# Recurrent gates of a two-block transformer kernel on one core: three products of rounded halves in place of one fp32 matmul

## The chip, the core and the metric

One core of a Trainium2 chip runs the whole program. It has five engines that work beside each other, each with its own queue of instructions, in order: TensorE (PE, matmul), VectorE (DVE), ScalarE (ACT), GpSimd (POOL) and SyncE (SP), the last two here used almost only to issue DMAs. The engines wait for each other by semaphores. The metric is the device time of one launch in microseconds (us), lower is better.

## The reference, cut to what matters

Two transformer blocks run over one sequence of 512 tokens and width 1024. The second one mixes tokens by dilated attention and by a gated linear recurrence of width 512, whose two gates are block-diagonal products (8 blocks of 64):

```python
def rg_lru(x, w_r, b_r, w_i, b_i, lam):
    xb = xf.reshape(b, s, N_LRU_BLOCKS, LRU_BLOCK)
    r = sigmoid(einsum('bsnc,ncd->bsnd', xb, w_r).reshape(b, s, c) + b_r)
    i = sigmoid(einsum('bsnc,ncd->bsnd', xb, w_i).reshape(b, s, c) + b_i)
    log_a = -LRU_C * r * softplus(-lam)
    a = exp(log_a)
    u = sqrt(-expm1(2.0 * log_a)) * (i * xf)
    _, h = associative_scan(combine, (a, u), axis=1)     # h = a * h_before + u
```

The input x of it is a projection of the normalised hidden state after a causal convolution of 4 taps. Everything is fp32.

## The kernel before, in words

Activations lie transposed: 128 features on the partitions, 512 tokens along them, so 1024 features are 8 such tiles. Weights stream from HBM in units of 128x1024 through a ring of four slots (`RING`). For each unit SyncE loads `w_raw`, ScalarE writes the rounded half `w_hi` and the negative of it, `w_lo` (lines 1025 and 1026, in `hi`, called by `ahead(name)` three units before the unit is used), and GpSimd adds `w_raw` onto `w_lo` by a DMA (line 514), so that `w_lo` is the remainder. Activations are split in the same way: ScalarE writes the rounded copy (type fp32r) and VectorE subtracts it from the source. `tile` (lines 545 to 547) then makes each fp32 product as three products of the rounded type: high by high, low by high, high by low. A tile of 8 pieces is 24 products into one of the two PSUM banks `pg`.

The stage of this case is the beginning of the second block's mixer. TensorE's order is written out by hand: the tiles xr0 to xr3 (512 recurrent features), each followed by the gate of the tile before it, then the attention tiles k2, q2, v2 of four head pairs with their scores. `lru_gate(t)` of TensorE (line 882) multiplies the convolved input `xc[:, t]` by a block-diagonal 128x128 piece for the r gate into bank `px` and by another for the i gate into bank `py`; both operands are plain fp32, and the matmul is not split. It waits for the third tap of the convolution (`xc_done`) and, on TensorE alone, for the weights of the gates (`l_landed`), which are 128x1024 (`lru_b`) and are loaded by a DMA from ScalarE's queue at line 1345, just ahead of the third norm's root.

Around it, for each t: VectorE multiplies the bank by the norm's root and frees it (line 1945), ScalarE makes the first tap (line 1357), VectorE the three others (line 1948). ScalarE's loop is at line 1354: the split of a later weight unit, the tap, and then, for t > 0, the sigmoids of gate t-1 (lines 1348 to 1352). The next `ahead` comes in the next turn of the loop. After gate 3 ScalarE and VectorE compute the factors and the scan (lines 1388 to 1393, 1951 to 1962), beside the first attention pair; `turn2` (line 904) is where TensorE needs VectorE's softmax of that pair. `statistic` (lines 599 to 606) sums squares for a norm. `put` (line 1474 of VectorE) adds a semaphore step to an instruction and has VectorE wait for it. SBUF buffers made in a closed `ExitStack` share their place with the ones made next.

Of the kernel before, what the change touches and what calls it, by code (L numbers as in the profile page):

```python
# [7 lines left out]
P = 128  # L8
T = 512
# [9 lines left out]
LRU_T = 512 // P  # L19
# [21 lines left out]
F32 = mybir.dt.float32  # L41
F32R = mybir.dt.float32r
BF16 = mybir.dt.bfloat16
ALU = mybir.AluOpType
ACT = mybir.ActivationFunctionType
# [148 lines left out]
def build(nc, weights, x_dram, consts, rope, masks, params, ssm_b, ssm_c, lru_w, out):  # L194
    with ExitStack() as ctx:
        def sb(name, shape, dt=F32, scope=ctx):
            return scope.enter_context(nc.sbuf_tensor(name, shape, dt))

        def sem(name):
            return ctx.enter_context(nc.semaphore(name))  # L200
# [72 lines left out]
        with ExitStack() as s:  # L273
            mx2_hi = sb("mx2_hi", [P, KT, T], F32R, scope=s)
            mx2_lo = sb("mx2_lo", [P, KT, T], F32R, scope=s)
            xc = sb("xc", [P, LRU_T, T], scope=s)
            tt = sb("tt", [P, LRU_T, T], scope=s)
            lru_b = sb("lru_b", [P, 2, LRU_T, P], scope=s)
            kk2 = sb("kk2", [P, 2, T], scope=s)
            qq2 = sb("qq2", [P, 2, T], scope=s)  # L280
            v_raw2 = sb("v_raw2", [P, T], scope=s)
            vv2 = sb("vv2", [P, QB, P], scope=s)
            prob2 = sb("prob2", [P, 6, T], scope=s)
            soft2 = sb("soft2", [P, 2, 8], scope=s)

# [56 lines left out]
        def psum(name, shape):  # L342
# [18 lines left out]
        c_landed, p_landed, s_landed, r_landed, l_landed, x2_landed = (  # L361
            sem(n) for n in ("c_landed", "p_landed", "s_landed", "r_landed", "l_landed", "x2_landed"))
# [14 lines left out]
        rs_k, rs_q, rs_o = sem("rs_k"), sem("rs_q"), sem("rs_o")  # L377
        cnv_act, silu_done, res_done = sem("cnv_act"), sem("silu_done"), sem("res_done")
        fin_mul, fin_pe, fin_act, fin_done = sem("fin_mul"), sem("fin_pe"), sem("fin_act"), sem("fin_done")
        xc_act, xc_done, la_done, tt_dve, tt_act, lru_h = (sem(n) for n in ("xc_act", "xc_done", "la_done", "tt_dve", "tt_act", "lru_h"))  # L380
        pv2_hi, cnv_done, gelu2_done, acc_done = sem("pv2_hi"), sem("cnv_done"), sem("gelu2_done"), sem("acc_done")

# [6 lines left out]
        def par(name, i=0):  # L389
            a, w = PARAMS[name]  # L390
            return prm[:, a + i:a + i + 1]

        def pars(name):
            a, w = PARAMS[name]
            return prm[:, a:a + w]
# [8 lines left out]
        def evacuated(eng, name):  # L404

            eng.wait_ge(pg_free[TILE[name] % 2], TILE[name] // 2 + 1)
# [10 lines left out]
        def ps_ready(eng, name):  # L417

            eng.wait_ge(ps_full, SUSE[name] + 1)
            return ps[SUSE[name] % 2]  # L420
# [107 lines left out]
        def _(pe):  # L528
# [242 lines left out]
            for h in range(1, HEADS + 2):  # L771
# [19 lines left out]
                if h >= 2:  # L791
# [4 lines left out]
                    for j in range(QB):  # L796
                        last = pe.matmul(py[:, P * j:T], vv[:, h % 2, j, :], pt[:, j, P * j:T],  # L797
                                         start=j == 0, stop=j == QB - 1)
# [83 lines left out]
            def lru_gate(t):  # L882
                for c, (bank, use, full, name) in enumerate(((px, x_use, px_full, "rg"), (py, y_use, py_full, "ig"))):
                    use((name, t))
                    if c == 0:
                        pe.wait_ge(xc_done, 3 * t + 3)
                        pe.wait_ge(l_landed, 16)
                    pe.matmul(bank[:], lru_b[:, c, t], xc[:, t], start=True, stop=True).then_inc(full, 1)

            for t in range(LRU_T):  # L890
                named(("xr", t), XH, XL, first_split=SPLIT["norm3"] if t == 0 else None, ahead_of=inside(3) if t == 0 else None)
                if t > 0:
                    lru_gate(t - 1)
# [39 lines left out]
            for j in range(PAIRS + 1):  # L933
                g = j - 1
                if j < PAIRS:
                    named(("k2", j), XH, XL)
                    if j == 0:
                        lru_gate(LRU_T - 1)
                    if j == 1:
                        value_turns(0)  # L940
# [67 lines left out]
        def _(act):  # L1008
            sent = {}

            def put(ins, s):

                ins.then_inc(s, 1)
                sent[s.name] = sent.get(s.name, 0) + 1
                return sent[s.name]
# [12 lines left out]
            def ahead(name):  # L1028
                hi(UNIT[name] + RING - 1)
# [8 lines left out]
            def px_ready(name):  # L1038
                act.wait_ge(px_full, XUSE[name] + 1)

            def py_ready(name):
                act.wait_ge(py_full, YUSE[name] + 1)
# [86 lines left out]
            for n, g in enumerate(GATES_FIRST):  # L1129
# [10 lines left out]
                if n == 10:  # L1140
                    for half in range(2):
                        use = ("y", half)
                        bank = ps_ready(act, use)
# [4 lines left out]
                if n == 11:  # L1148
                    for half in range(2):
                        use = ("yt", half)  # L1150
                        bank = ps_ready(act, use)
# [196 lines left out]
            def lru_gate(t):  # L1348
                px_ready(("rg", t))
                act.activation(ra[:, t], px[:], ACT.Sigmoid, bias=par("b_r", t)).then_inc(px_free, 1)  # L1350
                py_ready(("ig", t))
                act.activation(ii[:, t], py[:], ACT.Sigmoid, bias=par("b_i", t)).then_inc(py_free, 1)

            for t in range(LRU_T):
                ahead(("xr", t))
                evacuated(act, ("xr", t))
                put(act.activation(xc[:, t], sqr[:, t % 2], ACT.Identity, bias=par("cb2", t),
                                   scale=par("cw2", 12 + t)), xc_act)
                if t > 0:
                    lru_gate(t - 1)  # L1360

            def turned2(j, i):
                w = P * (i + 1)
                bank = ps_ready(act, ("t2", j, i))
                act.activation(pt2[i % 2][:, :, 0:i + 1, :], bank[:, :, 0:w].rearrange("p c (b q) -> p c b q", q=P), ACT.Copy)\
                    .then_inc(ps_free[SUSE[("t2", j, i)] % 2], 1)
# [106 lines left out]
        def _(dve):  # L1473
            sent = {}

            def put(ins, s):

                ins.then_inc(s, 1)
                sent[s.name] = sent.get(s.name, 0) + 1
                dve.wait_ge(s, sent[s.name])  # L1480
# [5 lines left out]
            def done(name):  # L1486
                dve.wait_ge(tile_done, TILE[name] + 1)
                return pg[TILE[name] % 2][:]

            def free(ins, name):  # L1490
                ins.then_inc(pg_free[TILE[name] % 2], 1)
                evacuated(dve, name)

            def tt_(out_, a, b, op=ALU.mult):
                return dve.tensor_tensor(out_, a, b, op)  # L1495

            def stt(out_, a, s, b, op0=ALU.mult, op1=ALU.mult):
                return dve.scalar_tensor_tensor(out_, a, s, b, op0, op1)  # L1498
# [442 lines left out]
            root_ready(3)  # L1941
            put(tt_(both[:], pars("mix_post"), pars("mlp_pre")), both_made)

            for t in range(LRU_T):
                free(tt_(sqr[:, t % 2], done(("xr", t)), rstd[:]), ("xr", t))
                dve.wait_ge(xc_act, t + 1)
                for d in (1, 2, 3):
                    put(stt(xc[:, t, d:T], sqr[:, t % 2, 0:T - d], par("cw2", 4 * (3 - d) + t), xc[:, t, d:T], ALU.mult,
                            ALU.add), xc_done)

            def lru_factor(t):

                dve.wait_ge(la_done, t + 1)
                link(tt_(nrm[:, t % 2], ra[:, t], ra[:, t]))
                put(stt(tt[:, t], nrm[:, t % 2], 1.0, tt[:, t], ALU.add, ALU.mult), tt_dve)
                py_read(dve, ("ig", t))
                link(tt_(ii[:, t], ii[:, t], xc[:, t]))
# [268 lines left out]
```

## Time and profile before

| | |
|---|---|
| median of 3 runs | 1428.45 us (1428.01 to 1429.33) |
| profiled execution | 1427.81 us |
| its span, first to last instruction | 1426.0 us |
| TensorE busy | 1402.4 us, 98% |
| ScalarE busy | 831.8 us, 58% |
| VectorE busy | 691.6 us, 48% |
| GpSimd busy | 197.7 us, 14% |
| mean DMA rate | 179 GB/s |

The profile is of one execution. The span is what its hardware profiler saw of instructions; 1.8 us of the execution's time lie around it. Matmuls are pipelined, so that the time of one row is longer than the distance to the next: the distance of two starts is what a matmul costs. An fp32 matmul appears as two instructions.

### The profile page before, as it was taken

To read this page: it belongs to the slowest core of one execution; us is meant where nothing else is said; L and a number is where in the kernel's file an instruction comes from. 1 tells how busy PE (TensorE), PEld (TensorE's weight loads), DVE (VectorE), ACT (ScalarE), POOL (GpSimd) and SP (SyncE) were. 2 spreads that over 40 slices of the span, in tenths; PEclk is the share of its full clock that TensorE was granted. 3 is DMA by queue.
4 is the path that set the end of the run, shared out by engine and by line. 5 is a ranking of instruction groups with operands and counts; after the bars stand their busy time and mean duration, and the time that the engine had idled before them with its cause. 6 is when DMAs were issued, how large, how long until landed. Compare 5 with 4: busy or idle time off the path is not lost.

```text
span 1426.0 us, 18304 instructions
## 1 busy us (share of the span) xinstructions
PE 1402.4 (98%) x6698; PEld 1118.5 (78%) x6698; DVE 691.6 (48%) x1211; ACT 831.8 (58%) x1169; POOL 197.7 (14%) x230
## 2 busy tenths in 40 slices
PE   7999999999999999999999999999999999999998
PEld 4887877777778888888888887777788888888885
DVE  6992567787733445554154164757464301212124
ACT  7546567776765665665355477645756655535442
POOL 1110110000111111111111111110101111111110
PEclk9999999999999999999999999999999999999999
DMA  9995976566479888888888996754667898988872
GB/s 295 199 209 152 209 168 146 126 154 142 115 186 230 188 195 190 194 190 198 203 186 187 216 239 151 159 140 110 144 152 162 192 208 180 201 198 181 203 161 85
DMA packets 81540, 254.76 MB, mean 179 GB/s; under 512 B 16688, under 2 KB 17840, under 8 KB 81456
## 3 DMA queue, kind: packets, MB, share of 16 engines
q0 software_dynamic: 32400, 117.98, 46.4%
q1 hardware_dynamic: 47616, 132.50, 30.7%
q10 hardware_dynamic: 1440, 3.15, 0.6%
q8 instruction: 54, 0.88, 0.2%
q14 instruction: 30, 0.25, 0.0%
HBM read 128.03 MB, written 3.41 MB: 92 GB/s over the span
## 4 chain that ended last, share of the span: by engine, by line
PE 93%; ACT 3%; DVE 3%; DMA 1%; issue 0%; SPq 0%; DVEq 0%; ACTq 0%
PE pg L545 27%; PE pg L547 27%; PE pg L546 27%; PE ps L719 2%; PE py L797 1%; PE ps L899 1%; PE ps L909 1%; ACT pairs_r L1189 1%; DMA w_raw<-weights 1%; PE py L919 1%; PE ps L721 0%; ACT kq_raw L1190 0%; PE ps L901 0%; DVE acc L1495 0%; DVE pairs L1495 0%
## 5 line engine op out<-in xcount | busy, mean ns | idle before, releaser
L545 PE MATMUL pg<-x_hi,w_hi 128*128 128x512 f32 x1088 | 429.2, 394 | 0.0
L547 PE MATMUL pg<-x_hi,w_lo 128*128 128x512 f32 x1088 | 424.2, 390 | 0.0
L546 PE MATMUL pg<-x_lo,w_hi 128*128 128x512 f32 x1088 | 423.7, 389 | 0.0
L514 POOL DMA_DIRECT2D w_lo<-w_raw x225 | 194.0, 862 | 1191.2 <-ACT w_lo L1026 1139.4
L1025 ACT ACTIVATE w_hi<-w_raw 128x1024 fp32r<-128x1024 f32 x222 | 233.4, 1051 | 107.6 <-PE pg L547 103.9
L545 PEld LDWEIGHTS pg<-x_hi,w_hi 128*128 128x128 f32 x1088 | 204.4, 188 | 43.2 <-issue 1.6
L547 PEld LDWEIGHTS pg<-x_hi,w_lo 128*128 128x128 f32 x1088 | 204.3, 188 | 42.9
L546 PEld LDWEIGHTS pg<-x_lo,w_hi 128*128 128x128 f32 x1088 | 204.5, 188 | 42.6 <-issue 1.0
L1026 ACT ACTIVATE w_lo<-w_raw 128x1024 fp32r<-128x1024 f32 x222 | 232.2, 1046 | 0.0
L547 PE MATMUL pg<-act_hi,w_lo 128*128 128x512 f32 x432 | 168.2, 389 | 0.0
L546 PE MATMUL pg<-act_lo,w_hi 128*128 128x512 f32 x432 | 168.1, 389 | 0.0
L545 PE MATMUL pg<-act_hi,w_hi 128*128 128x512 f32 x432 | 168.1, 389 | 0.0
L546 PEld LDWEIGHTS pg<-act_lo,w_hi 128*128 128x128 f32 x432 | 81.1, 188 | 16.9
L545 PEld LDWEIGHTS pg<-act_hi,w_hi 128*128 128x128 f32 x432 | 81.1, 188 | 16.8
L547 PEld LDWEIGHTS pg<-act_hi,w_lo 128*128 128x128 f32 x432 | 81.1, 188 | 16.7
L1495 DVE TENSOR_TENSOR pairs<-rel 128x512 f32<-128x512 f32 x30 | 20.8, 692 | 134.5 <-ACT rel L1448 134.5
L1495 DVE TENSOR_TENSOR cu<-pg,rstd 128x512 f32<-128x512 f32 x44 | 30.4, 692 | 114.6 <-PE pg L547 112.9
L1495 DVE TENSOR_TENSOR hid<-hid,pg 128x512 f32<-128x512 f32 x32 | 22.0, 688 | 102.8 <-PE pg L547 98.3
L1498 DVE SCALAR_TENSOR_TENSOR cnv<-cu,prm,cnv 128x511 f32<-128x511 f32 x88 | 66.1, 751 | 3.1
L1495 DVE TENSOR_TENSOR acc<-acc,pg 128x512 f32<-128x512 f32 x24 | 16.5, 688 | 96.1 <-PE pg L547 96.1
L1169 ACT ACTIVATE pr<-ps,soft 128x128 f32<-128x128 f32 (+3 forms) x64 | 33.2, 523 | 27.2 <-DVE soft L1779 26.5
L1779 DVE TENSOR_REDUCE soft<-ps 128x2 f32<-128x256 f32 (+3 forms) x48 | 39.6, 824 | 6.7 <-PE ps L901 4.1
(355 smaller groups left out, 1711.7 us busy)
## 6 DMA issues: line engine op xcount, KB each, us to landing
w_raw<-weights SPq DMA_DIRECT2D x226, 512.0 KB, 5.0
w_lo<-w_raw POOLq DMA_DIRECT2D x225, 512.0 KB, 5.8
kq_rot<-kq_raw SPq DMA_DIRECT2D x64, 64.0 KB, 3.1
hid<-x SPq DMA_DIRECT2D x4, 512.0 KB, 5.5
hid<-x ACTq DMA_DIRECT2D x8, 256.0 KB, 5.3
out<-hid SPq DMA_DIRECT2D x8, 256.0 KB, 2.2
u_dram<-hid SPq DMA_DIRECT2D x4, 256.0 KB, 5.2
pairs<-u_dram SPq DMA_DIRECT2D x8, 128.0 KB, 8.1
```

What stands on the lines that cost most here:

```text
L514: pool.dma_start(w_lo[:, s], w_raw[:, s], accum_op=ALU.add).then_inc(lo_in[s], 16)
L545: pe.matmul(bank[:], wh, xh(k), start=n == 0, stop=False)
L546: pe.matmul(bank[:], wh, xl(k), start=False, stop=False)
L547: last = pe.matmul(bank[:], wl, xh(k), start=False, stop=n == len(ks) - 1)
L719: pe.matmul(bank[:, c, 0:w], qq[r, h % 2, P * i:P * i + P], kk[r, h % 2, 0:w], start=True, stop=False)
L797: last = pe.matmul(py[:, P * j:T], vv[:, h % 2, j, :], pt[:, j, P * j:T], start=j == 0, stop=j == QB - 1)
L1025: act.activation(w_hi[:, s], w_raw[:, s], ACT.Copy)
L1026: put(act.activation(w_lo[:, s], w_raw[:, s], ACT.Copy, scale=-1.0), hi_done)
L1169: ins = act.activation(dst[:, c, 0:w], bank[:, c, 0:w], ACT.Exp, bias=negmax[:, i % 2, c:c + 1], **kw)
L1495: return dve.tensor_tensor(out_, a, b, op)
L1498: return dve.scalar_tensor_tensor(out_, a, s, b, op0, op1)
L1779: put(dve.tensor_reduce(s[:, i % 2, 0:2], bank[:, :, 0:w], AX.X, ALU.max, negate=True), maxed)
```

## The change

It adds split halves of the gate weights, `lb_hi` (rounded copy, ScalarE) and `lb_lo` (remainder, VectorE), made once ahead of the loop over t, and split halves of the gate input, `xc_hi` and `xc_lo`, made for each t in two alternating buffers. The four fit into places of buffers that are filled later (`qq2`, `prob2`). TensorE's gate is three products of the rounded type for each of r and i. `wait_ge(l_landed, 16)` moves from TensorE to ScalarE, ahead of `lb_hi`; VectorE waits for `lb_hi` ahead of its evacuation of xr0; ScalarE waits for the third tap of each t ahead of `xc_hi`, and VectorE for `xc_hi` ahead of `xc_lo`, which TensorE waits for.

```diff
--- before.py
+++ after.py
@@ -277,9 +277,15 @@
             tt = sb("tt", [P, LRU_T, T], scope=s)
             lru_b = sb("lru_b", [P, 2, LRU_T, P], scope=s)
             kk2 = sb("kk2", [P, 2, T], scope=s)
+            with ExitStack() as s2:
+                lb_lo = sb("lb_lo", [P, 2, LRU_T, P], F32R, scope=s2)
             qq2 = sb("qq2", [P, 2, T], scope=s)
             v_raw2 = sb("v_raw2", [P, T], scope=s)
             vv2 = sb("vv2", [P, QB, P], scope=s)
+            with ExitStack() as s2:
+                xc_hi = sb("xc_hi", [P, 2, T], F32R, scope=s2)
+                xc_lo = sb("xc_lo", [P, 2, T], F32R, scope=s2)
+                lb_hi = sb("lb_hi", [P, 2, LRU_T, P], F32R, scope=s2)
             prob2 = sb("prob2", [P, 6, T], scope=s)
             soft2 = sb("soft2", [P, 2, 8], scope=s)
 
@@ -377,6 +383,7 @@
         rs_k, rs_q, rs_o = sem("rs_k"), sem("rs_q"), sem("rs_o")
         cnv_act, silu_done, res_done = sem("cnv_act"), sem("silu_done"), sem("res_done")
         fin_mul, fin_pe, fin_act, fin_done = sem("fin_mul"), sem("fin_pe"), sem("fin_act"), sem("fin_done")
+        lb_high, lb_low, xc_high, xc_low = sem("lb_high"), sem("lb_low"), sem("xc_high"), sem("xc_low")
         xc_act, xc_done, la_done, tt_dve, tt_act, lru_h = (sem(n) for n in ("xc_act", "xc_done", "la_done", "tt_dve", "tt_act", "lru_h"))
         pv2_hi, cnv_done, gelu2_done, acc_done = sem("pv2_hi"), sem("cnv_done"), sem("gelu2_done"), sem("acc_done")
 
@@ -883,9 +890,11 @@
                 for c, (bank, use, full, name) in enumerate(((px, x_use, px_full, "rg"), (py, y_use, py_full, "ig"))):
                     use((name, t))
                     if c == 0:
-                        pe.wait_ge(xc_done, 3 * t + 3)
-                        pe.wait_ge(l_landed, 16)
-                    pe.matmul(bank[:], lru_b[:, c, t], xc[:, t], start=True, stop=True).then_inc(full, 1)
+                        pe.wait_ge(lb_low, 1)
+                        pe.wait_ge(xc_low, t + 1)
+                    pe.matmul(bank[:], lb_hi[:, c, t], xc_hi[:, t % 2], start=True, stop=False)
+                    pe.matmul(bank[:], lb_hi[:, c, t], xc_lo[:, t % 2], start=False, stop=False)
+                    pe.matmul(bank[:], lb_lo[:, c, t], xc_hi[:, t % 2], start=False, stop=True).then_inc(full, 1)
 
             for t in range(LRU_T):
                 named(("xr", t), XH, XL, first_split=SPLIT["norm3"] if t == 0 else None, ahead_of=inside(3) if t == 0 else None)
@@ -1351,6 +1360,8 @@
                 py_ready(("ig", t))
                 act.activation(ii[:, t], py[:], ACT.Sigmoid, bias=par("b_i", t)).then_inc(py_free, 1)
 
+            act.wait_ge(l_landed, 16)
+            put(act.activation(lb_hi[:], lru_b[:], ACT.Copy), lb_high)
             for t in range(LRU_T):
                 ahead(("xr", t))
                 evacuated(act, ("xr", t))
@@ -1358,6 +1369,8 @@
                                    scale=par("cw2", 12 + t)), xc_act)
                 if t > 0:
                     lru_gate(t - 1)
+                act.wait_ge(xc_done, 3 * t + 3)
+                put(act.activation(xc_hi[:, t % 2], xc[:, t], ACT.Copy), xc_high)
 
             def turned2(j, i):
                 w = P * (i + 1)
@@ -1941,12 +1954,16 @@
             root_ready(3)
             put(tt_(both[:], pars("mix_post"), pars("mlp_pre")), both_made)
 
+            dve.wait_ge(lb_high, 1)
+            put(tt_(lb_lo[:], lru_b[:], lb_hi[:].bitcast(F32), ALU.subtract), lb_low)
             for t in range(LRU_T):
                 free(tt_(sqr[:, t % 2], done(("xr", t)), rstd[:]), ("xr", t))
                 dve.wait_ge(xc_act, t + 1)
                 for d in (1, 2, 3):
                     put(stt(xc[:, t, d:T], sqr[:, t % 2, 0:T - d], par("cw2", 4 * (3 - d) + t), xc[:, t, d:T], ALU.mult,
                             ALU.add), xc_done)
+                dve.wait_ge(xc_high, t + 1)
+                put(tt_(xc_lo[:, t % 2], xc[:, t], xc_hi[:, t % 2].bitcast(F32), ALU.subtract), xc_low)
 
             def lru_factor(t):
```

## Rows read from the trace of the kernel before

**Rows 1.** one line of the page, part 1: busy us, share, instructions.

```profile
PE 1402.4 (98%) x6698; PEld 1118.5 (78%) x6698; DVE 691.6 (48%) x1211; ACT 831.8 (58%) x1169; POOL 197.7 (14%) x230
```

**Rows 2.** the page, part 4: the chain that ended last.

```profile
PE 93%; ACT 3%; DVE 3%; DMA 1%; issue 0%; SPq 0%; DVEq 0%; ACTq 0%
PE pg L545 27%; PE pg L547 27%; PE pg L546 27%; PE ps L719 2%; PE py L797 1%; PE ps L899 1%; PE ps L909 1%; ACT pairs_r L1189 1%; DMA w_raw<-weights 1%; PE py L919 1%; PE ps L721 0%; ACT kq_raw L1190 0%; PE ps L901 0%; DVE acc L1495 0%; DVE pairs L1495 0%
```

**Rows 3.** timeline of TensorE: start us, us, engine, line, [idle before].

```profile
855.63 0.39 PE L546 MATMUL pg<-x_lo,w_hi 128*128 128x512 f32 x1
855.86 0.39 PE L547 MATMUL pg<-x_hi,w_lo 128*128 128x512 f32 x1
856.09 1.02 PE L888 MATMUL px<-xc,lru_b 128*128 128x512 f32 x2
...
863.30 1.02 PE L888 MATMUL px<-xc,lru_b 128*128 128x512 f32 x2
```

**Rows 4.** timeline of ScalarE, same columns.

```profile
850.18 0.63 ACT L1074 ACTIVATE rstd<-rstd 128x512 f32<-128x512 f32 x1
850.72 1.04 ACT L1025 ACTIVATE w_hi<-w_raw 128x1024 fp32r<-128x1024 f32 x1
851.66 1.04 ACT L1026 ACTIVATE w_lo<-w_raw 128x1024 fp32r<-128x1024 f32 x1
...
857.09 0.81 ACT L1357 ACTIVATE xc<-pairs,prm 128x512 f32<-128x512 f32 x1 [1.77 <-DVE pairs L1495]
857.92 1.28 ACT L1350 ACT_TABLE_LOAD   x1
859.21 0.69 ACT L1350 ACTIVATE acc<-px,prm 128x512 f32<-128x512 f32 x1
```

**Rows 5.** timeline of VectorE, same columns.

```profile
847.88 0.69 DVE L1495 TENSOR_TENSOR pairs_r<-rstd,pairs_r 128x512 fp32r<-128x512 f32 x1
...
851.11 0.69 DVE L1495 TENSOR_TENSOR pairs<-pg,rstd 128x512 f32<-128x512 f32 x1
853.51 2.32 DVE L1498 SCALAR_TENSOR_TENSOR xc<-pairs,prm,xc 128x511 f32<-128x511 f32 x3 [1.71 <-ACT xc L1357]
...
858.00 2.32 DVE L1498 SCALAR_TENSOR_TENSOR xc<-pairs,prm,xc 128x511 f32<-128x511 f32 x3 [0.95 <-ACT xc L1357]
```

**Rows 6.** load of the gate weights: timeline of ScalarE's queue, view of line 1345.

```profile
847.16 0.33 ACTq L1345 DMA_DIRECT2D lru_b<-lru_w  x1
...
DMA to landing us min/median/max: 5.7/5.7/5.7
```

**Rows 7.** the view of line 1558: duration ns min/median/max, start, shape.

```profile
L1558 DVE TENSOR_TENSOR w_lo<-w_raw,w_hi x1: 1224/1224/1224, 12.7 to 12.7; 128x1024 fp32r<-128x1024 f32 x1
```

**Rows 8.** timeline of both engines at the recurrent split.

```profile
923.79 0.63 ACT L1047 ACTIVATE mx_hi<-pairs 128x512 fp32r<-128x512 f32 x1 [0.83 <-DVE pairs L1495]
...
924.53 0.69 DVE L1495 TENSOR_TENSOR mx_lo<-pairs,mx_hi 128x512 fp32r<-128x512 f32 x1 [0.77 <-ACT mx_hi L1047]
```

**Rows 9.** timeline of TensorE at the third norm's sum.

```profile
848.72 0.47 PE L604 MATMUL px<-pairs_r,blocks 128*128 128x512 f32 x1 [0.33 <-DVE pairs_r L1495]
849.02 0.40 PE L605 MATMUL px<-pairs_r,blocks 128*128 128x512 f32 x1
```

**Rows 10.** the view of w_lo: its 225 additions by DMA.

```profile
DMA to landing us min/median/max: 4.5/5.8/12.0
```

**Rows 11.** waits of TensorE: us in total, times, longest.

```profile
PE ps L909 <- DVE prob L1501: 0.7, 1, 0.7
```

**Rows 12.** timeline of TensorE at the start.

```profile
11.39 1.02 PE L622 MATMUL px<-gates 128*128 128x512 f32 x2
...
17.00 0.77 PE L561 MATMUL pg<-x_hi,w_hi 128*128 128x512 f32 x1 [2.65 <-DVE x_lo L1495]
```

**Rows 13.** stretches at the start: busy us by engine, then granted clock, DMA share.

```profile
12.50:16.00 3.50, 0.35 (x2) 0.30 (x2) 2.76 (x4) 2.85 (x7) 0.00 (x0) 1.00 1.04 415
16.10:22.80 6.70, 5.80 (x14) 4.57 (x15) 6.39 (x10) 6.70 (x11) 1.86 (x2) 0.50 1.05 311
```

## The prediction

> **What bounds the kernel now.** I read the busy times first: TensorE is busy for 1402.4 of 1426.0 us [rows 1]. The chain that ended last says the same: 93% of it is TensorE, 81 of the 93 on the three lines that multiply by streamed weights, 3% is ScalarE and 3% VectorE [rows 2]. So a microsecond of matmul taken out of TensorE's queue is worth a microsecond, and a microsecond in which TensorE is made to wait costs one. The other two views are therefore TensorE's own order of instructions around the gates, and the order on ScalarE and VectorE that leads up to the first gate. TensorE runs tile xr0, tile xr1, gate 0, tile xr2, gate 1, tile xr3, gate 2, tile k2_0, gate 3. The last product of xr1 is issued at 855.86, gate 0 follows at 856.09 with no idle time [rows 3]. That this works is close: the third convolution tap of t = 0 starts at 853.51 + 2 steps and ends at 853.51 + 2.32 = 855.83 [rows 5], 0.26 us before the gate wants it. Gates 1 to 3 have room: the taps of t = 1 end at 858.00 + 2.32 = 860.32 and gate 1 starts at 863.30 [rows 3, 5].
>
> **What the matmuls give back.** One period from gate 0 to gate 1 is 863.30 - 856.09 = 7.21 us [rows 3]. In it lie the 24 products of one tile. Neighbouring products are 0.227 us apart (855.63, 855.86, 856.09) [rows 3], so the tile takes 24 x 0.227 = 5.45 us and the fp32 gate 1.76 us (two fp32 matmuls, each two instructions). The new gate is six products of the kind of the tile: 6 x 0.227 = 1.36 us. Saved: 0.40 us per gate, four gates, 1.6 us, all on the path while TensorE doesn't wait. The rule of the Trainium skill (FP8 and Floating Point Precision, TensorE Precision Notes) is that a true fp32 product is four passes, high and low halves each with each; three of four would save 1.76 / 4 x 4 = 1.8 us. The rows give 1.6, and I go by them; an instruction pair per matmul in the trace doesn't contradict it.
>
> **What the splits cost, step by step, for t = 0.** This is where the change can hurt, since before it gate 0 had 0.26 us of slack and four new operations and one new wait now stand ahead of it in series. I lay them out in time, taking everything up to the third root (exponential done at 850.81 [rows 4]) as unchanged.
> - *The wait for the gate weights.* Before, only TensorE waited for `l_landed`, at 856. Now ScalarE does, directly behind the root, and everything later in its queue stands behind it. The transfer is issued at 847.16 and lands 5.7 us later, at 852.86 [rows 6]. ScalarE, which before went on at 850.72 with the weights of the next tile [rows 4], idles for 2.1 us. Queued behind are the split of two weight tiles, the first tap and the gates' sigmoids.
> - *lb_hi*, 128x1024 on ScalarE: the same shape as the weight copy, 1.04 us [rows 4]: 852.86 to 853.91.
> - *The weight copies of ahead(xr0)*, 0.95 us apart [rows 4]: to about 855.85. They finish before the first tap has its input, so they cost nothing here.
> - *lb_lo*, 128x1024 on VectorE: the one such operation in the trace took 1224 ns [rows 7]; with 0.1 us of handover from ScalarE, 854.0 to 855.25. VectorE stands at it from 851.1 on, and queued behind it is the evacuation of xr0, which before ran at 851.11 [rows 5].
> - *Evacuation*, 0.69: to 855.97. *First tap on ScalarE* and its handover: 857.09 to 858.00 in the row of t = 1 [rows 4, 5], 0.91: VectorE's taps start at 856.93. *Three taps*, 2.32: to 859.25.
> - *xc_hi on ScalarE, xc_lo on VectorE.* The nearest pair is the split of the recurrent output: ScalarE starts at 923.79, VectorE at 924.53 for 0.69 [rows 8]. From the end of the taps: 0.04 + 0.74 + 0.69 = 1.47: to 860.72. TensorE starts 0.15 behind such an end (847.88 + 0.69 = 848.57, matmul at 848.72) [rows 5, 9].
>
> So gate 0 starts at 860.9 in place of 856.1: TensorE stands for 4.8 us where it stood for none. To this I add 0.1 us for the slower first products behind a wait (848.72 to 849.02, 0.30 in place of 0.23) [rows 9]. Of the 4.9 the wait for the transfer carries 2.1: had the gate weights been there at 850.81, the same steps would begin and end 2.05 us earlier and gate 0 would start at 858.8.
>
> **The later gates.** t = 1 on ScalarE: xc_hi(0) ends at 859.95, then the weight copies to 861.95, the tap (its input from VectorE is ready at 861.6) with handover to 862.85, VectorE's taps to 865.2, the pair to 866.65, TensorE ready at 866.8. TensorE ends gate 0 at 860.9 + 1.4 = 862.3 and xr2 at 867.75. 0.9 us of slack. The sigmoids of gate 0 with their table load, 1.28 + twice 0.69 [rows 4], run from 862.75 to 865.3, beside the taps, and xc_hi(1) is queued just behind them; the slack holds this. For t = 2 and 3 the input comes when the tile ends, and from there to its own gate VectorE and ScalarE need 0.7 (evacuation) + 0.9 (tap, handover) + 2.3 (taps) + 1.5 (the pair) + 0.15 = 5.6 us. TensorE meanwhile has the gate before, 1.36, and the next tile, 5.45, which is 6.8: 1.2 us of slack. Without that cover each gate would wait by the difference.
>
> **Weights, DMA queues.** ScalarE's delay moves the split of xr3's weights from 852.7 to 855.85 and that of k2_0's from 855.3 to 861.95. GpSimd issues the addition behind each, SyncE the next load behind that. An addition lands after 5.8 us in the median and 12.0 at most [rows 10]: xr3's at 862 to 868, wanted at 869.2; k2_0's at 868 to 874, wanted at 876. No cost, but at the far end 1 us of room only.
>
> **Downstream.** Behind gate 3 the chain goes over ScalarE and VectorE to the turns of the first pair, where TensorE waits 0.70 us [rows 11]. That chain begins with the sigmoids of gate 3, which move with TensorE (gate 3 is 0.4 us shorter for both sides), so that wait stays as it is: it neither swallows the new stall nor grows. The reuse of the two buffers of xc_hi and xc_lo is two gates apart and waits for nothing.
>
> **The sum.** 4.9 - 1.6 = +3.3 us. The profiled execution took 1427.81 us, 1.8 around its span of 1426.0; by it, 1431.1. The median of the runs shown is 0.6 above it, 1428.45, which gives 1431.8. Bounds of the unshown parts: landing 0.5 us earlier or later (it shares the DMA engines with weight traffic), handovers 0.3 us in all, which makes 2.5 to 4.2 us.
>
> **Rival one: the clock falls in the gap.** TensorE's granted clock is full everywhere in this part. The one place where the trace shows it fall is the start. The last 512-column matmul there begins its pair at 11.39 and ends at 12.41, then come two short ones, busy for 0.35 us together, and real work starts at 17.00 [rows 12, 13]. The granted clock is 1.00 up to 16.0 and 0.50 from 16.1 to 22.8, though TensorE was busy for 5.8 of these 6.7 us [rows 13], that is at 1.2 of 2.4 GHz. This cost half of 5.8, 2.9 us. The new gap of 4.8 us is as long as that one (4.6) and emptier. Against it: one instance only, behind a thin start, and here the engine was fully busy up to the gap. If it falls, the price is from near 0 to 3.3 us, by how much of the slow stretch lies inside the gap; I take the row's 2.9, which gives 1431.8 + 2.9 = 1434.6. It hides nowhere, since TensorE is the bound. The Trainium skill (TensorE: Matmul & The Clock Gate, HAM oscillation — how this bites in real kernels) has the rule that idle gaps between bursts of matmuls send the clock to its lower level and the next burst starts cold; the start of this trace agrees.
>
> **Rival two, on the other side: the gap isn't there and the kernel is faster.** The mechanism would be that the data of gate 0 are ready by 856.1, so that the 1.6 us of matmul time is all that is left: 1428.45 - 1.6 = 1426.9. It decides from a chain shorter by 4.8 us; the landing can give 2.1, and the rest would need two of the four new operations to overlap, which their semaphores don't allow. What speaks for it is only that the landing is a single row.
>
> **Rival three: the transfer lands early.** If ScalarE finds the gate weights there at 850.81, the stall is 2.7 + 0.1 and the change +1.2 us: 1429.6, no change that can be told. That asks for 3.7 us, while the additions, of the same 512 KB, never took less than 4.5 [rows 10], so it isn't likely.
>
> **How the numbers follow.** A measurement of this kernel can tell some 0.2%, 2.9 us, from no change, so 1431.3 is the border. The stall with the clock kept, 1431.8 (1430.9 to 1432.7): 0.46; of it three quarters lie over the border, 0.34, and 0.12 under. The stall with the clock falling, 1434.6 (1432 to 1435.6): 0.38, all over. Early landing, 1429.6: 0.10, same. No gap, 1426.9: 0.06, faster or same by half. Slower 0.72, same 0.25, faster 0.03. The range leaves out the no-gap case and half of the early landing: 1430.1 to 1435.4.
>
> **What would show it.** Right: a row of TensorE's gate matmul with idle time of 4 to 5 us ahead of it at t = 0 and none at t = 1 to 3; lb_hi on ScalarE starting at 852.9 with the landing as its releaser; gate periods of 5.45 + 1.36 = 6.8 us in place of 7.21; the 0.70 us wait of the first turn unchanged. The clock: the mean granted clock of the stretch behind the gap, and products 0.43 us apart there. Wrong: a second stall at gate 1 (ScalarE's queue fuller than laid out), a wait for weights at xr3 or k2_0, or a chain that TensorE doesn't stand for.

## The result, and the profile after

| | before | changed |
|---|---|---|
| median of 5 runs | 1428.15 us (1427.66 to 1429.33) | 1435.09 us (1433.31 to 1436.51) |
| profiled execution, span | 1427.81, 1426.0 | 1435.09, 1433.3 |
| ratio to before | | 1.0046, 95% interval 1.0036 to 1.0057 |

The change makes the kernel 6.9 us slower. The forecast of 1431.8 had the sign and the place, and its range of 1430.1 to 1435.4 holds the median, but the size was half of what came. The measured value is that of the first rival, 1434.6: the gap with the clock falling in it. How far that agreement is luck is said further down.

The page of the changed kernel, the busy time of TensorE and the chain that ended last (before in rows 1 and 2). Lines 545 to 547 of before are now 552 to 554, ScalarE's and VectorE's lines move too:

```profile
PE 1402.6 (98%) x6702; PEld 1120.1 (78%) x6706; DVE 695.3 (49%) x1216; ACT 835.5 (58%) x1174; POOL 197.7 (14%) x230
...
PE 90%; ACT 4%; DVE 3%; DMA 2%; issue 1%; SPq 0%; DVEq 0%; ACTq 0%
PE pg L552 27%; PE pg L554 26%; PE pg L553 26%; PE ps L726 2%; PE py L804 1%; PE ps L908 1%; PE ps L918 1%; ACT pairs_r L1198 1%; DMA w_raw<-weights 1%; DMA w_lo<-w_raw 1%; PE py L928 1%; DMA lru_b<-lru_w 0%; PE ps L728 0%; ACT kq_raw L1199 0%; DVE pairs L1508 0%
```

TensorE is busy for 0.2 us more than before although eight fp32 matmuls (two for each gate) have become cheaper. The busy time counts slow work and much work alike, so the saving and the slow clock cancel in it. Its share of the chain is down from 93% [rows 2] to 90%, and the load of the gate weights has appeared in the chain. Where it stands shows in TensorE's order around the gates (timeline, columns as in rows 3):

```profile
856.46 0.39 PE L554 MATMUL pg<-x_hi,w_lo 128*128 128x512 f32 x1
862.73 0.77 PE L895 MATMUL px<-xc_hi,lb_hi 128*128 128x512 f32 x1 [5.88 <-DVE xc_lo L1508]
863.29 0.63 PE L896 MATMUL px<-xc_lo,lb_hi 128*128 128x512 f32 x1
...
866.71 0.62 PE L552 MATMUL pg<-x_hi,w_hi 128*128 128x512 f32 x1
867.13 0.42 PE L553 MATMUL pg<-x_lo,w_hi 128*128 128x512 f32 x1
867.40 0.39 PE L554 MATMUL pg<-x_hi,w_lo 128*128 128x512 f32 x1
...
871.75 0.39 PE L895 MATMUL px<-xc_hi,lb_hi 128*128 128x512 f32 x1
...
878.54 0.39 PE L895 MATMUL px<-xc_hi,lb_hi 128*128 128x512 f32 x1
```

The last product of xr1 starts at 856.46 and gate 0 at 862.73: 5.88 us of idle time, where there was none [rows 3]. The six products of the gate and the first five of xr2 behind it are 0.43 us apart (as 866.71 to 867.13; the first step, 862.73 to 863.29, is longer still); after one step of 0.27 they are 0.23 apart again. From 862.73 to 867.40 there are 11 steps in 4.67 us, where 11 x 0.227 would be 2.50: 2.2 us lost. Gate 1 and gate 2 start at 871.75 and 878.54 without a wait, 6.79 us apart where it was 7.21 [rows 3].

Stretches of the changed kernel (busy us of each engine, then the granted clock, DMA share, GB/s), the gap's first half, the stretch behind and the one after:

```profile
857.00:860.00 3.00, 0.00 (x0) 0.00 (x0) 1.98 (x4) 1.50 (x2) 0.86 (x1) 1.00 0.23 44
860.50:867.20 6.70, 4.47 (x11) 3.55 (x12) 4.26 (x6) 6.01 (x8) 0.86 (x1) 0.50 0.74 168
867.50:874.00 6.50, 6.50 (x30) 5.34 (x29) 1.73 (x3) 3.14 (x4) 0.86 (x1) 1.00 0.68 153
```

The granted clock is 1.00 for the first part of the gap, 0.50 from 860.5 to 867.2, 1.00 after: 1.2 in place of 2.4 GHz. So it fell some 4 us after the last product of xr1 was issued, inside the gap, and 4.5 us of work ran at it. Before the change the only such stretch was at the start [rows 13].

Why gate 0 is late, from ScalarE's and VectorE's timelines of the changed kernel:

```profile
847.75 0.34 ACTq L1354 DMA_DIRECT2D lru_b<-lru_w  x1
...
850.76 0.63 ACT L1083 ACTIVATE rstd<-rstd 128x512 f32<-128x512 f32 x1
854.74 1.06 ACT L1364 ACTIVATE lb_hi<-lru_b 128x1024 fp32r<-128x1024 f32 x1 [3.34 <-DMA lru_b<-lru_w]
855.71 1.04 ACT L1034 ACTIVATE w_hi<-w_raw 128x1024 fp32r<-128x1024 f32 x1
856.65 1.04 ACT L1035 ACTIVATE w_lo<-w_raw 128x1024 fp32r<-128x1024 f32 x1
857.89 0.81 ACT L1368 ACTIVATE xc<-pairs,prm 128x512 f32<-128x512 f32 x1 [0.20 <-DVE pairs L1508]
861.16 0.63 ACT L1373 ACTIVATE xc_hi<-xc 128x512 fp32r<-128x512 f32 x1 [2.46 <-DVE xc L1511]
```

```profile
855.90 1.23 DVE L1508 TENSOR_TENSOR lb_lo<-lru_b,lb_hi 128x1024 fp32r<-128x1024 f32 x1 [4.24 <-ACT lb_hi L1364]
857.16 0.69 DVE L1508 TENSOR_TENSOR pairs<-pg,rstd 128x512 f32<-128x512 f32 x1
858.80 2.32 DVE L1511 SCALAR_TENSOR_TENSOR xc<-pairs,prm,xc 128x511 f32<-128x511 f32 x3 [0.95 <-ACT xc L1368]
861.89 0.69 DVE L1508 TENSOR_TENSOR xc_lo<-xc,xc_hi 128x512 fp32r<-128x512 f32 x1 [0.77 <-ACT xc_hi L1373]
```

These are the steps of the forecast in their order: the root ends at 851.39, ScalarE idles for 3.34 us until the gate weights land; then come lb_hi, lb_lo, the evacuation of xr0, the taps, xc_hi and xc_lo. The one step that differs in size is the first, the landing. The load was issued at 847.75 and took this long (view of its line):

```profile
DMA to landing us min/median/max: 7.0/7.0/7.0
```

7.0 us, where the trace of before had 5.7 [rows 6].

TensorE's waits in the changed kernel, in total, times and longest:

```profile
PE px L895 <- DVE xc_lo L1508: 5.9, 1, 5.9
...
PE ps L918 <- DVE prob L1514: 0.7, 1, 0.7
...
PE pg L552 <- DMA w_lo<-w_raw: 0.5, 1, 0.5
```

The wait of the first turn, 0.7 us, is what it was [rows 11]. A wait of 0.5 us for an addition to `w_lo` is new, but it lies at 836.44, ahead of anything that the change touches. Two kernels below that are the same as before up to this point have a wait of 0.6 us there too, so it comes and goes between executions. It accounts for most of the 0.6 us by which the starts near 850 are late against before. The span then adds up: 6.0 (856.69 to 862.73) + 2.2 (clock) - 1.6 (four times 0.4) + 0.5 = 7.1, measured 1433.3 - 1426.0 = 7.3.

### The profile page after: what moved, and what is told of

Read it like the earlier page. It is cut to its first block, busy times and chain, and to the rows that moved or that the text cites. A ratio compares the mean times of both kernels' runs of the same rounds, so it can differ in the third digit from the quotient of the medians.

```text
span 1433.3 us, 18331 instructions
## 1 busy us (share of the span) xinstructions
PE 1402.6 (98%) x6702; PEld 1120.1 (78%) x6706; DVE 695.3 (49%) x1216; ACT 835.5 (58%) x1174; POOL 197.7 (14%) x230
## 4 chain that ended last, share of the span: by engine, by line
PE 90%; ACT 4%; DVE 3%; DMA 2%; issue 1%; SPq 0%; DVEq 0%; ACTq 0%
PE pg L552 27%; PE pg L554 26%; PE pg L553 26%; PE ps L726 2%; PE py L804 1%; PE ps L908 1%; PE ps L918 1%; ACT pairs_r L1198 1%; DMA w_raw<-weights 1%; DMA w_lo<-w_raw 1%; PE py L928 1%; DMA lru_b<-lru_w 0%; PE ps L728 0%; ACT kq_raw L1199 0%; DVE pairs L1508 0%
```

## The experiments

The theory after the result had three terms: three products for one fp32 matmul save 1.6 us; a gap before gate 0 costs 6 us, of which the wait for the gate weights is over half and the series of splits the rest; the clock falls in the gap and costs 2.2 us more. The rivals: the products save nothing in place; the landing is hidden and the splits alone make the gap; the clock falls for another reason or its fall costs nothing. What the nine kernels gave is below. Landing, gap and clock are those of one profiled execution each (landing: issue to landing of the gate weights; gap: end of xr1's last product to the start of gate 0). The last column is the median of before from the same group of runs; each ratio further down is against it.

| kernel | landing, us | gap, us | clock behind the gap | median, us | before beside it |
|---|---|---|---|---|---|
| before | 5.7 | 0 | full | 1428.15 | |
| changed | 7.0 | 6.0 | half | 1435.09 | 1428.15 |
| changed, again | 7.5 | 6.6 | half | 1435.45 | 1428.11 |
| products alone | 6.8 | 0 | full | 1426.51 | 1428.06 |
| wait alone | 7.1 | 3.4 | half | 1433.74 | 1428.06 |
| splits alone | 7.8 | 6.9 | half | 1437.06 | 1428.11 |
| gap filled | 7.5 | 6.6, 4.6 of it filled | full | 1432.67 | 1428.06 |
| load early | in time | 2.6 | full | 1429.10 | 1428.06 |
| splits early | in time | 1.2 | full | 1427.65 | 1428.11 |
| splits early, gate 0 later | in time | 0 | full | 1426.44 | 1428.11 |

**Products alone.** Before, with the products of the gates on other operands:

```diff
-                    pe.matmul(bank[:], lru_b[:, c, t], xc[:, t], start=True, stop=True).then_inc(full, 1)
+                    wt, xt = blocks[:, c], x_hi[:, t]
+                    pe.matmul(bank[:], wt, xt, start=True, stop=False)
+                    pe.matmul(bank[:], wt, xt, start=False, stop=False)
+                    pe.matmul(bank[:], wt, xt, start=False, stop=True).then_inc(full, 1)
```

> The kernel before, with each fp32 gate matmul replaced by three products of the rounded type on other tiles that are already rounded (the ones tile and x_hi); the gates are not computed, the waits are those of before. It prices the matmul part alone. Theory: gate period 5.45 + 1.36 = 6.81 us in place of 7.21, no stall, so 1.6 us less than before: 1426.5. Rival (the three products are no cheaper in place, for example because each brings its own weight load and the fp32 one hides it): 1428.1, period 7.2.

Measured: 1426.51 (1425.78 to 1427.40, 11 runs) against 1428.06, ratio 0.9989, interval 0.9980 to 0.9998. Its timeline of TensorE has the gates at

```profile
857.00 0.39 PE L889 MATMUL px<-x_hi,blocks 128*128 128x512 f32 x1
...
863.83 0.39 PE L889 MATMUL px<-x_hi,blocks 128*128 128x512 f32 x1
```

6.83 us apart, and there is no wait for a gate. The saving is 1.55 us as summed. The rival falls: its period was 7.2, and its time, that of before, lies just outside the interval.

**The wait alone.** Before, plus one line on ScalarE:

```diff
             inverse_root(3, rstd)
 ...
+            act.wait_ge(l_landed, 16)
             for t in range(LRU_T):
                 ahead(("xr", t))
```

> The kernel before, with nothing but a wait for the gate weights added on ScalarE ahead of its loop over the recurrent tiles; no split is made and the fp32 gates stay. Theory that the landing is a main part of the stall: ScalarE idles 2 to 3.3 us, tap 0 is late by as much, TensorE stands 1.9 to 3.2 us ahead of gate 0 (0.26 us of slack taken off, 0.8 us gained or lost by the weight copies), 1430 to 1431.5, clock kept. Rival (the split operations alone make the stall, the landing is hidden): within 0.3 us of before.

Measured: 1433.74 (1431.25 to 1434.51), ratio 1.0036, interval 1.0022 to 1.0049. The landing isn't hidden; the wait alone costs 5.7 us, more than I had expected. ScalarE's timeline:

```profile
855.00 1.06 ACT L1025 ACTIVATE w_hi<-w_raw 128x1024 fp32r<-128x1024 f32 x1 [3.46 <-DMA lru_b<-lru_w]
...
856.92 0.80 ACT L1358 ACTIVATE xc<-pairs,prm 128x512 f32<-128x512 f32 x1
```

TensorE's:

```profile
856.60 0.39 PE L547 MATMUL pg<-x_hi,w_lo 128*128 128x512 f32 x1
860.24 2.02 PE L888 MATMUL px<-xc,lru_b 128*128 128x512 f32 x2 [3.25 <-issue]
...
863.96 0.39 PE L546 MATMUL pg<-x_lo,w_hi 128*128 128x512 f32 x1
```

The weight copies that stood at 850.72 [rows 4] start at 855.00 and the first tap at 856.92. The gap is 856.83 to 860.24, 3.4 us, with a landing of 7.1; 3.2 was the most that was expected. The larger miss is the clock, which I had taken as kept: from 860.24 to 863.96 the gate and one product take 3.72 us, where the same took 858.03 - 856.09 = 1.94 in the kernel before [rows 3], whose second product of xr2 is

```profile
858.03 0.40 PE L546 MATMUL pg<-x_lo,w_hi 128*128 128x512 f32 x1
```

3.4 + 1.8 = 5.2. The rest of this execution's 5.9 us (its span is 1431.9) is mostly a wait of 0.6 us for an addition at 836.55, as in the changed kernel. So a gap of 3.4 us was long enough here to meet the fall. The five runs lie in two places: 1431.3 and 1431.8, where the gap with a full clock would put them (1428.06 + 3.4 = 1431.5), and 1433.7 to 1434.5. That the clock was kept in the lower two is likely but not shown; only a run of the upper group has a trace.

**The gap filled.** The changed kernel, with work that nobody reads ahead of gate 0's wait:

```diff
                     use((name, t))
+                    if c == 0 and t == 0:
+                        for _ in range(20):
+                            pe.matmul(bank[:], blocks[:, 0], x_hi[:, 0], start=True, stop=True)
                     if c == 0:
                         pe.wait_ge(lb_low, 1)
```

> The changed kernel, with 20 products of 0.227 us (4.5 us in all) on tiles at hand put ahead of the first gate's wait, into the gate's own bank, where the first gate overwrites them: TensorE works in the gap and the gap's end isn't moved. Theory that the gap makes the granted clock fall: the clock stays full, products behind the gate stay 0.227 us apart, 1435.1 - 2.3 = 1432.8. Rival (the clock falls for another reason, or its fall costs nothing because the next gate waits anyway): 1435.1.

Measured: 1432.67 (1431.31 to 1433.36, 7 runs), ratio 1.0033, interval 1.0021 to 1.0044. TensorE's timeline and the stretches:

```profile
855.86 4.70 PE L894 MATMUL px<-x_hi,blocks 128*128 128x512 f32 x20
862.42 0.47 PE L898 MATMUL px<-xc_hi,lb_hi 128*128 128x512 f32 x1 [1.86 <-DVE xc_lo L1511]
862.72 0.40 PE L899 MATMUL px<-xc_lo,lb_hi 128*128 128x512 f32 x1
```

```profile
856.00:862.00 6.00, 4.55 (x21) 3.43 (x19) 4.18 (x6) 3.35 (x5) 0.86 (x1) 1.00 0.46 87
862.40:869.00 6.60, 6.58 (x29) 5.50 (x30) 3.54 (x5) 6.57 (x9) 0.86 (x1) 1.00 0.70 159
```

Gate 0 is as late as in the changed kernel (862.42, and here the gate weights took 7.5 us), but the clock is 1.00 throughout, and the gate's products are 0.30 and then 0.23 apart. 2.4 us come back by adding 20 matmuls (2.8 against the second measurement of the changed kernel, whose gap is as long, 6.6 us). All seven runs are at or below 1433.36, all ten of the changed kernel at or above 1433.31. This shows that it is the idle time that lets the clock fall, and that the fall costs 2.4 to 2.8 us by the medians. The sum for the changed kernel agrees: 1428.15 + 6.0 + 2.2 - 1.6 = 1434.8, measured 1435.09.

This is also the case in which gate 1 stands under a full clock: its xc_lo ends at 867.97 and it starts at 869.31 without a wait. The slack that the forecast gave the later gates is there, and not a gift of the slow clock.

**The load early.** The changed kernel, with the DMA moved to the first of the last eight tiles of the feed-forward:

```diff
                             evacuated(act, ("down", c, m))
+                            if m == 0:
+                                act.dma_start(lru_b[:], lru_w).then_inc(l_landed, 16)
                             square(3, m, hid[:, m])
 ...
-            act.dma_start(lru_b[:], lru_w).then_inc(l_landed, 16)
             inverse_root(3, rstd)
```

> The changed kernel, with the load of the gate weights issued some 30 us earlier, behind the first of the last eight tiles of the feed-forward, so that ScalarE never waits for it. Theory: lb_hi starts at about 850.8, the gap before gate 0 is 2.7 us, the clock is kept: 1428.2 + 2.8 - 1.6 = 1429.4. Rival (the gap comes from the chain of splits, and an earlier landing only moves the wait): gap near 6 us, 1435.

Measured: 1429.10 (1428.62 to 1430.80, 11 runs), ratio 1.0010, interval 1.0001 to 1.0019. ScalarE and TensorE:

```profile
850.14 0.63 ACT L1083 ACTIVATE rstd<-rstd 128x512 f32<-128x512 f32 x1
850.68 1.04 ACT L1365 ACTIVATE lb_hi<-lru_b 128x1024 fp32r<-128x1024 f32 x1
```

```profile
855.83 0.39 PE L554 MATMUL pg<-x_hi,w_lo 128*128 128x512 f32 x1
858.65 0.47 PE L895 MATMUL px<-xc_hi,lb_hi 128*128 128x512 f32 x1 [2.43 <-DVE xc_lo L1509]
```

lb_hi follows the root with no wait, the idle time is 2.43 us, and no product is slow in this execution. One moved DMA takes back 5.9 of the 6.9 us: 3.4 us of gap and the clock's 2.2 account for 5.6. The forecast's third rival had put this case at 1429.6 by the same steps.

**The splits of the weights early.** As the last, with lb_hi behind the fourth and lb_lo behind the fifth of those eight tiles:

```diff
                             split_hi("norm3", m, x_hi[:, m], nrm[:, m % 2])
+                            if m == 3:
+                                act.wait_ge(l_landed, 16)
+                                put(act.activation(lb_hi[:], lru_b[:], ACT.Copy), lb_high)
 ...
                             scaled("norm3", m, "mix_pre", 3)
+                            if m == 4:
+                                dve.wait_ge(lb_high, 1)
+                                put(tt_(lb_lo[:], lru_b[:], lb_hi[:].bitcast(F32), ALU.subtract), lb_low)
```

> The changed kernel with the load of the gate weights and both their splits moved ahead, in among the last eight tiles of the feed-forward; only the split of the gate input is left on the way to gate 0. Theory: VectorE evacuates xr0 at 851.1 as before the change, tap 0 stays at 852.6, the taps end at 855.8 and the split adds 1.5 + 0.15, so a gap of 1.4 us: 1428.1 + 1.4 - 1.6 = 1427.9. Rival (the splits of the weights delay the norm's operations among which they now stand): a new wait at the third norm's sum or at xr0 of 0.5 to 2 us, 1428.5 to 1430.

Measured: 1427.65 (1427.29 to 1428.21, 11 runs), ratio 0.9996, interval 0.9987 to 1.0005. TensorE's waits between 800 and 870 us:

```profile
PE px L895 <- DVE xc_lo L1510: 1.2, 1, 1.2
PE px L611 <- DVE pairs_r L1510: 0.3, 1, 0.3
```

1.2 us are left ahead of gate 0, the price of splitting its input; the wait at the third norm's sum is the 0.3 us of before [rows 9], so the moved work costs nothing where it stands now. In time this kernel can't be told from before (the interval holds 1.0): the gap takes most of what the products save.

**Gate 0 later.** As the last, and gate 0 inside tile xr2:

```diff
-                named(("xr", t), XH, XL, first_split=SPLIT["norm3"] if t == 0 else None, ahead_of=inside(3) if t == 0 else None)
-                if t > 0:
+                named(("xr", t), XH, XL, first_split=SPLIT["norm3"] if t == 0 else None,
+                      ahead_of=inside(3) if t == 0 else (lambda k: lru_gate(0) if k == 3 else None) if t == 2 else None)
+                if t > 1:
                     lru_gate(t - 1)
```

> As the one with early splits, and gate 0 is issued behind the ninth product of tile xr2 in place of ahead of it: 9 x 0.227 = 2.0 us of work lie between the end of xr1 and the gate, more than the remaining 1.4 us. Theory: no gap, all of the 1.6 us comes out: 1426.5, as with the products alone. Rival (switching between two accumulations or the later sigmoids on ScalarE cost it again at gate 1): 1427.5 or more, with a wait at gate 1.

Measured: 1426.44 (1426.03 to 1427.44, 11 runs), ratio 0.9987, interval 0.9978 to 0.9996. It is faster than both kernels and stands where the products alone stood. TensorE's waits between 800 and 870 us, then gate 0, the remainder that gate 1 needs, and gate 1:

```profile
PE px L611 <- DVE pairs_r L1511: 0.3, 1, 0.3
```

```profile
857.81 0.39 PE L895 MATMUL px<-xc_hi,lb_hi 128*128 128x512 f32 x1
...
862.02 0.69 DVE L1511 TENSOR_TENSOR xc_lo<-xc,xc_hi 128x512 fp32r<-128x512 f32 x1 [0.78 <-ACT xc_hi L1376]
...
862.86 0.47 PE L895 MATMUL px<-xc_hi,lb_hi 128*128 128x512 f32 x1
```

No wait for a gate is listed. Gate 1 starts at 862.86, though 15 products of xr2 and the six of gate 0 end at 857.81 + 21 x 0.227 = 862.58: 0.3 us are lost there. The remainder xc_lo of gate 1 ends at 862.71, 0.15 us ahead of the gate, so this is a short wait for it that the list doesn't show: with gate 0 later and no gap, gate 1 has no slack left. It is the rival's wait, but 0.3 us where the rival had 1 us or more.

**The splits alone.** The changed kernel, with the fp32 matmul put back and all waits kept:

```diff
-                    pe.matmul(bank[:], lb_hi[:, c, t], xc_hi[:, t % 2], start=True, stop=False)
-                    pe.matmul(bank[:], lb_hi[:, c, t], xc_lo[:, t % 2], start=False, stop=False)
-                    pe.matmul(bank[:], lb_lo[:, c, t], xc_hi[:, t % 2], start=False, stop=True).then_inc(full, 1)
+                    pe.matmul(bank[:], lru_b[:, c, t], xc[:, t], start=True, stop=True).then_inc(full, 1)
```

> The changed kernel with its fp32 gate matmul put back: all splits and waits stay, TensorE still waits for the low halves, but multiplies the unsplit tiles. Theory (the matmul part is worth 1.6 us and independent of the gap): 1435.1 + 1.6 = 1436.7, a gap of some 6 us ahead of gate 0, the clock falling in most executions. Rival (with the longer fp32 gates the later stages have the cover that the three products lack, so that part of the loss goes away): 1435 or less.

Measured: 1437.06 (1434.29 to 1438.19), ratio 1.0056, interval 1.0042 to 1.0070. TensorE at gate 0:

```profile
863.51 2.04 PE L895 MATMUL px<-xc,lru_b 128*128 128x512 f32 x2 [6.76 <-DVE xc_lo L1506]
```

1.6 to 2.0 us above the changed kernel, with a gap 0.9 us longer than its profile's. The spread of five runs is 4 us, so this agrees with 1.6 without fixing it.

**The changed kernel again.**

> The changed kernel once more, beside the others. Theory: its load of the gate weights lands in about 7 us, not in the 5.7 of the first trace of before (7.0 in the changed kernel, 7.1 and 7.5 in two others), so the gap is 5.5 to 6.5 us again and the time 1433 to 1436.5, lower where the clock is kept. Rival (5.7 is typical and the changed kernel's trace was the exception): a gap of 4.8 and 1432 to 1434.

Measured: 1435.45 (1435.14 to 1436.30), ratio 1.0050, interval 1.0036 to 1.0064. The landing, and TensorE's waits:

```profile
DMA to landing us min/median/max: 7.5/7.5/7.5
```

```profile
PE px L895 <- DVE xc_lo L1508: 6.5, 1, 6.5
```

7.5 us, with a wait of 6.5, and a wait of 0.8 us for an addition at 837 us. Of the seven traces in which the load stands at its old place, before's 5.7 is the shortest; the others are 6.8, 7.0, 7.1, 7.5, 7.5 and 7.8.

## Why the prediction was right or wrong

- **TensorE is the bound, and a gap on it costs its length: right.** Every kernel of the table follows from before, minus 1.6 for the products, plus its gap, plus the clock's 2 us where it fell, to within 0.6 us.
- **1.6 us saved by the products: right.** 1.55 measured alone, gate periods of 6.79 in place of 7.21. The sum by the four passes of the Trainium skill (FP8 and Floating Point Precision, TensorE Precision Notes), 1.8, is further off than the rows' 1.6, though the interval (0.3 to 2.9 us) doesn't part them.
- **The gap, 4.8 us forecast and 6.0 measured: the mechanism and every step right, one term mis-sized.** From the landing to gate 0 the forecast had 8.0 us (852.86 to 860.9) and the trace has 7.99 (854.74 to 862.73). The term that was off is the landing itself: 5.7 us, read from a single row, measured 7.0. The bound of half a microsecond that I put on it was a guess, and no row of before carried it: the same trace showed additions of the same size between 4.5 and 12.0 us [rows 10], which should have widened it. (The bounds themselves add up to 4.1 us at the upper end, not 4.2.)
- **The clock kept as the likeliest case, 0.46 against 0.38: wrong.** The row of the start [rows 12, 13] was the right one to read for whether the clock falls: a gap as long, and the clock fell in it. I discounted it as a single instance with little work ahead of it. In the changed kernel it fell with 24-product tiles ahead, in both of its profiles, and with the wait alone even in a gap of 3.4 us. The rule of the Trainium skill named there (TensorE: Matmul & The Clock Gate, HAM oscillation: idle gaps between bursts of matmuls let the clock fall) holds in this trace: 0.50 behind a gap of 6 us.
- **The price of the fall, 2.9: wrong as a reading, near by luck.** Half of the busy time in the slow stretch is what the clock took from the products, not what it took from the kernel. At the start the two differ. A row of before, then two of the changed kernel, then the changed kernel's slow stretch at the start:

```profile
28.55 0.50 PE L561 MATMUL pg<-x_hi,w_hi 128*128 128x512 f32 x1
```

```profile
16.80 0.47 PE L568 MATMUL pg<-x_hi,w_hi 128*128 128x512 f32 x1 [2.65 <-DVE x_lo L1508]
...
28.34 0.50 PE L568 MATMUL pg<-x_hi,w_hi 128*128 128x512 f32 x1 [0.34 <-DVE x_lo L1508]
```

```profile
17.30:20.70 3.40, 3.40 (x9) 2.66 (x8) 3.23 (x6) 3.40 (x5) 1.47 (x2) 0.50 1.07 352
```

The slow stretch is 3.4 us long here and 6.7 in before [rows 13], yet from the first product (17.00 [rows 12], here 16.80) to the same product further on it takes 11.55 us in before and 11.54 here: with the shorter stretch TensorE waits for VectorE's x_lo instead. There the longer stretch cost nothing more. At gate 0, where TensorE is the bound, half of the slow work counts: the stretch has the same length, 6.7 us, of which 2.2 lie inside the gap, and half of the other 4.5 is the 2.2 that the steps show. That rival one's 1434.6 comes within 0.5 us of the measured time is luck in part: its gap was 1.2 us too short, its price of the clock 0.7 too high, and it started from 1428.45 where the median of five runs is 1428.15.
- **No second stall at gates 1 to 3, none for weights, the turn's 0.7 us unchanged: right.** Gate 1 waits for nothing, with the slow clock (which gave ScalarE and VectorE more room) and with the full one (the gap filled).
- **The third rival, an early landing, 1429.6: measured as a kernel, 1429.1.** The second, no gap, 1426.9: 1426.4 once the load, the splits and the gate had been moved.
- **The chances.** 0.72 for slower was deserved, the point was low: both misses, 1.2 us of gap and 2.2 us of clock, go the same way. They are hardly independent: among the traces with a gap before gate 0 left unfilled the clock fell in those of 3.4 us and more and was kept in those of 1.2 and 2.6. The range held the median by 0.3 us only.

## What to carry to other kernels

A wait that is moved to an engine earlier in the chain must be costed with the spread of the transfer that it waits for, not with the one landing in the trace, above all where it was loose before and nothing showed its margin. On a kernel bound by TensorE, price a new gap twice: its length, and the slow products behind it (seen here from gaps of 3.4 us up); filling it with throw-away products shows the second part by itself. Read that second part only from a place where TensorE is the bound: at the start of this kernel a slow stretch twice as long cost no more. A cheaper operation that needs prepared operands pays only when the preparation is off the path: here one load issued 30 us earlier, two splits moved and one gate issued nine products later turn +6.9 us into -1.7.

## What the runs showed of the hardware

- The load of 512 KB from ScalarE's queue took 6.9 to 7.1 us in the three traces in which it was issued near 816 us too; 5.7 was the exception, not the later 7 to 7.8.
- The granted clock fell to half in or at the end of the gaps of 3.4, 6.0, 6.6 and 6.9 us before gate 0, and not in the profiles with 1.2 or 2.6 us or with 6.6 us of which 4.6 were filled.
- At the start of the program, behind the gap of rows 12, it fell at 16.1 in before, ahead of the first product of 17.00, but at 17.3 in the changed kernel and 18.0 in the load early, 0.5 and 1.1 us after work had begun again. So where in or behind a gap it falls differs between executions, and so does how much work runs slow.
- Whether it falls in a gap of one size seems to differ too, but no two traces of one kernel show it. The five runs of the changed kernel have mean clocks of 0.998 (1433.31 us) and 0.995 to 0.996 (1434.57 to 1436.51). Of the eleven with a gap of 2.6 us, two at 0.996 took 1430.6 and 1430.8 us, against 1429.1 in the median; but three at 0.998 took 1430.0 to 1430.4, so the clock doesn't explain all of the spread. What decides it wasn't tried.
